# Expert rows gathered and scattered over 128 partitions instead of 96, with the slots permuted

## The chip, the cores and the metric

The kernel runs on one core of a Trainium2 chip. The metric is the device time of one execution in microseconds (us). Engines are named as in the profile: PE (TensorE), DVE (VectorE), ACT (ScalarE), POOL (GpSimd) and SP (SyncE, which here only issues DMAs). A core has 16 DMA engines; DMAs that SP issues go over one queue (q1, hardware), those of GpSimd over another (q0, software).

## What is computed

One step of a decoder layer: sparse attention and pooling over 528 prompt rows and 8 sample rows, then a mixture of experts. The change touches only the experts. 520 rows (tokens) of 1024 float32 values go to 4 of 32 experts each, so an expert gets 65 rows on average:

```python
logits = (x @ w_router).astype(jnp.float32) + b_router.astype(jnp.float32)
top_v, top_e = lax.top_k(logits, TOP_EXPERTS)          # 4 of 32
gates = jax.nn.softmax(top_v, axis=-1)
...
gu = xe @ w_gu[e] + b_gu[e]                            # 1024 -> 2048
gate = jnp.minimum(gu[:, :D_EXPERT], SWIGLU_LIMIT)
up = jnp.clip(gu[:, D_EXPERT:], -SWIGLU_LIMIT, SWIGLU_LIMIT)
act = (up + 1.0) * gate * jax.nn.sigmoid(SWIGLU_ALPHA * gate)
return act @ w_down[e] + b_down[e]
...
y = jnp.zeros((N + 1, D_MODEL), jnp.float32).at[slot_tok].add(yb.astype(jnp.float32) * slot_gate[:, None])[:N]
```

Everything is float32. The weights of one expert are 12 MB (six ring loads of 2048 KB).

## The kernel before, in words

The instructions of each engine are written out by hand, one function per engine, and tied by semaphores (`S[...]`). After attention and the output projection, the normalised rows lie in memory as `h_rows`, and the residual rows, to which the experts' results are added, as `y_acc`. Then the 32 experts follow one another; two sets of buffers (`u` = 0, 1) alternate.

**Slots.** An expert has room for 96 rows (`CAP`) in 128 slots (`SLOTS`): `iota_b` holds, for each column, which place in the expert's list that column stands for; columns 96 to 127 repeat places 64 to 95. `compare` (VectorE) sets `iota_b` against the place of each token in the expert's list, and `pick` (PE, L1250) multiplies the result with token numbers and gates, so that each partition gets the token number and the gate of its slot. `slot_rows` makes the row index out of it (`idx_i`, partitions 0 to 95); an unused slot gets an index above 519. Places are handed out from 0 up, so an expert with 65 tokens fills slots 0 to 64.

**Rows.** `gather` (POOL, L640) fetches the rows of `h_rows` for the next expert, `xg[u][0:96]`, skipping indices above 519. `turn_rows` (VectorE, L1672) turns them to `hTe`, the stationary operand. The result, `ysc[u][0:96]`, is added to `y_acc` by an indirect DMA with addition (POOL, L657), with the indices that `keep` has saved as `idx_y`. The last expert is not scattered but added by a matmul with `back` (`last_rows`, from `idx_f`). The first gather stands alone ahead of the first expert, and PE turns its rows (`turn_rows_first`, L1280).

**One expert on PE** (`pair`): `gu_round` three times (gate and up columns, L1294), with `pick` for the next expert behind the first round; two transposes (L1327, L1338); `down_wide` and `down_rest` (L1301, L1307). The groups of slots in a round are 32 wide: group 0 is partitions 0 to 31, group 1 32 to 63, group 2 64 to 95; the fourth quarter of a bank computes other columns for group 2, and so needs the gates of group 2 on partitions 96 to 127 as well.

**SP's queue** (`load`) issues, in the order in which PE sets the ring slots free: ring slots 0 and 1 (or `ring_more`), 2, 3, then the bias rows of the next expert, then slots 4 and 5. The bias rows go to four partitions, 6 KB each, L444:

```python
sp.dma_start(b_rows[0:P:GRP, :], b_gu[bass.ds(e, 1)].rearrange("a j x -> (a j) x")).then_inc(S["b_rows_in"], 16)
```

On VectorE, `pair` begins with the wait for these bias rows, and the comparison for the next expert stands behind it:

```python
dve.wait_ge(S["b_rows_in"], (ne + 1) * 16)
compare(e + 1, 1 - u)
```

and on PE `pick` waits for `cmp_ready` of that comparison before the second round can start.

Of the kernel before, what the change touches and what calls it, by code (L numbers as in the profile page):

```python
# [21 lines left out]
ALU = mybir.AluOpType  # L22
# [5 lines left out]
P = 128  # L28
# [6 lines left out]
NQ = NT - META  # L35
# [14 lines left out]
CAP = 96  # L50
SLOTS = 128
GRP = 32
# [23 lines left out]
def build_step(nc, xT, xnat, consts, g_mix, w_mt, w_v, w_mix, pool_scale, w_bra, w_brp, w_out,  # L76
# [4 lines left out]
    with ctx:  # L81
        def sb(name, shape, dt=F32):
            return ctx.enter_context(nc.sbuf_tensor(name, shape, dt))

        def sem(name):
            return ctx.enter_context(nc.semaphore(name))

        def dram(name, shape, dt=F32):
            return nc.dram_tensor(name, shape, dt).ap()

        y_acc = dram("y_acc", (NQ + CAP, D))
        h_rows = dram("h_rows", (NQ + CAP, D))
# [21 lines left out]
        idx_i = [sb(f"idx_i{n}", [P, 1], I32) for n in range(2)]  # L114
        idx_y = [sb(f"idx_y{n}", [P, 1], I32) for n in range(2)]
# [18 lines left out]
        def part(region, at, *shape):  # L134
            n = int(np.prod(shape))
            v = region[:, at:at + n]
            names = "abcd"[:len(shape)]
            if len(shape) == 1:
                return v
            return v.rearrange(f"p ({' '.join(names)}) -> p {' '.join(names)}", **dict(zip(names[1:], shape[1:])))  # L140
# [6 lines left out]
        iota96 = cst[:, C_IOTA:C_IOTA + CAP]  # L147
# [67 lines left out]
        def xn(t):  # L215
            return part(QK, D * t, D) if t < 4 else part(VN, 0, D)
# [22 lines left out]
        xg = [part(X1, D * n, D) for n in range(2)]  # L239
        ysc = [part(X1, D * (2 + n), D) for n in range(2)]  # L240
# [4 lines left out]
        iota_b = part(XR, 2048, SLOTS)  # L245
# [32 lines left out]
        def bank(n, w=512, at=0):  # L278
            return PSF[:, 512 * n + at:512 * n + at + w]
# [33 lines left out]
        scat = [sem(f"scattered{n}") for n in range(2)]  # L313
# [24 lines left out]
        def link(eng, ins, name, count):  # L338

            count[0] += 1  # L340
            ins.then_inc(S[name], 1)
            eng.wait_ge(S[name], count[0])
# [173 lines left out]
        def _(po):  # L516
# [120 lines left out]
            def gather(b, e, u):  # L637
                po.wait_ge(S["idx_ready"], b * SELS + e + 1)
                po.sem_inc(S["may"], 1)
                po.indirect_dma_start(xg[u][0:CAP], None, h_rows, bass.IndirectOffsetOnAxis(ap=idx_i[u][0:CAP, :], axis=0),  # L640
                                      bounds_check=NQ - 1, oob_is_err=False)\
                    .then_inc(gath[u], 16)

            def pair(b, i, first=False, last=False):
                for u in range(2):
                    e = i * 2 + u
                    gather(b, e + 1, 1 - u)
                    if u == 0:
                        po.wait_ge(scat[1], (b * (NE // 2) + i + (1 if first else 0)) * 16)
                    else:  # L650
                        po.wait_ge(scat[0], (b * (NE // 2) + i + 2) * 16)
                    if last and u == 1:
                        continue
                    po.wait_ge(S["idx_kept"], b * SELS + e + 1)
                    po.wait_ge(S["y_ready"], b * NE + e + 2)
                    po.sem_inc(S["may"], 1)
                    po.indirect_dma_start(y_acc, bass.IndirectOffsetOnAxis(ap=idx_y[u][0:CAP, :], axis=0),  # L657
                                          ysc[u][0:CAP], None, bounds_check=NQ - 1, oob_is_err=False, compute_op=ALU.add).then_inc(scat[u], 16)

            def experts(b, first=False):  # L660
                gather(b, 0, 0)
# [5 lines left out]
            def last_pair():  # L667
                pair(0, NE // 2 - 1, True, True)
# [718 lines left out]
        def _(dve):  # L1387
            n = [0]
            L = lambda ins: link(dve, ins, "dve_step", n)
# [149 lines left out]
            def norm_rows(n):  # L1539
                t = WO_ORDER[n]  # L1540
                r = TROWS[t]
                dve.wait_ge(S["row_ms"], 2 * n + 2)
                L(dve.reciprocal(rms[0:r, t:t + 1], rms[0:r, t:t + 1]))
                dve.scalar_tensor_tensor(out=hf(t)[0:r], in0=xn(t)[0:r], scalar=rms[0:r, t:t + 1], in1=gffn[0:r],
                                         op0=ALU.mult, op1=ALU.mult).then_inc(S["hf_done"], 1)
# [29 lines left out]
            for o, t in enumerate(WO_ORDER):  # L1575
                j, r = J_WO + o, TROWS[t]
                dve.wait_ge(S["proj_done"], j + 1)
                if t < 4:
                    x1 = xn(t).rearrange("p (a b) -> p a b", a=2)
                    dve.tensor_tensor(x1, PB[j % 2], x1, ALU.add).then_inc(S["dve_taken"], 1)  # L1580
                else:
                    for q in range(3):
                        x1 = xn(t)[0:r, 256 * q:256 * q + 256]
                        dve.tensor_tensor(x1, PB[j % 2][32 * q:32 * q + r, 0, 0:256], x1, ALU.add)
                    x1 = xn(t)[0:r, 768:D]
                    dve.tensor_tensor(x1, PB[j % 2][96:96 + r, 0, 0:256], x1, ALU.add).then_inc(S["dve_taken"], 1)
                if o == 0:
                    dve.wait_ge(S["late_in"], 48)
                    L(dve.memset(rt_log, 0.0))
                    L(dve.memset(posv, -1.0))  # L1590
                    L(dve.memset(gx, 0.0))
                    L(dve.tensor_copy(gx[:, :, 0:NE, 0], tokid[:, 0:1].unsqueeze(2).broadcast_to([P, NTILE, NE])))
                    for t_ in range(1, NTILE):
                        L(dve.memset(gx[:, t_, 0:NE, 1], float(t_)))
                    L(dve.memset(gx[:, :, 0:NE, 2], 1.0))
                if o == NTILE - 1:
                    L(dve.tensor_copy(iota_b[:, 0:CAP], iota96))
                    L(dve.tensor_copy(iota_b[:, CAP:SLOTS], iota96[:, 64:CAP]))
                norm_rows(o)
                for m in ((), (), (0,), (1,), (2, 3))[o]:  # L1600
                    find(m)
                    add_before(m)
# [6 lines left out]
            def gates():  # L1609
                dve.tensor_tensor(rt_w, top_v[:, :, 0:TOPE], top_v[:, :, 0:1].broadcast_to([P, NTILE, TOPE]), ALU.subtract).then_inc(S["sel_ready"], 1)  # L1610
                slot_rows(1, 0)
                add_before(NTILE - 1)
                dve.wait_ge(S["sel_ready"], 2)
                L(dve.tensor_reduce(sum4, rt_w, AX.X, ALU.add))
                L(dve.reciprocal(sum4, sum4))
                L(dve.tensor_tensor(rt_w, rt_w, sum4.unsqueeze(2).broadcast_to([P, NTILE, TOPE]), ALU.mult))
                L(dve.tensor_tensor(rt_eg, rt_eq, rt_w.unsqueeze(3).broadcast_to([P, NTILE, TOPE, NE]), ALU.mult))
                dve.tensor_reduce(rt_g, rt_eg.rearrange("p t k e -> p t e k"), AX.X, ALU.add).then_inc(S["g_ready"], 1)
                dve.wait_ge(S["g_ready"], 1)
                L(dve.tensor_copy(gx[:, :, 0:NE, 3], rt_g))  # L1620
                L(dve.tensor_tensor(rt_eg[:, :, 1, :], rt_g, gx[:, :, 0:NE, 3], ALU.subtract))
                L(dve.tensor_copy(gx[:, :, 0:NE, 4], rt_eg[:, :, 1, :]))
                dve.tensor_tensor(gx[:, :, 0:NE, 5], rt_eg[:, :, 1, :], gx[:, :, 0:NE, 4], ALU.subtract).then_inc(S["gx_ready"], 1)
                dve.wait_ge(S["acc_init"], 16 * 2 * NTILE)
                dve.memset(b_rows, 0.0).then_inc(S["zero_late"], 1)
                dve.memset(act_t[1][64:P], 0.0).then_inc(S["zero_late"], 1)
                dve.wait_ge(S["gate_picked"], 1)
                dve.tensor_reduce(gcol[0], bank(RANK, 3, 200), AX.X, ALU.add).then_inc(S["gcol_set"], 1)
                L(dve.tensor_reduce(rt_cnt[0:1, 0:1], bank(RANK, NE, NE * NTILE)[0:1], AX.X, ALU.max))
                dve.tensor_copy(cnt_i[0:1, 0:1], rt_cnt[0:1, 0:1]).then_inc(S["cnt_ready"], 1)  # L1630
                dve.wait_ge(S["gT_turned"], 1)
                dve.tensor_copy(back[CAP:P, 0:4, :], bank(2)[CAP:P].rearrange("p (t x) -> p t x", t=4))
                dve.tensor_copy(back[CAP:P, 4, :], bank(7, P)[CAP:P]).then_inc(S["gT_done"], 1)
                dve.tensor_copy(iota_row[:, 0:CAP], iota96)
                L(dve.tensor_scalar(iota_row[:, CAP:P], iota96[:, 0:P - CAP], float(CAP), None, ALU.add))
# [246 lines left out]
```

## Time and profile before

| what | value |
|---|---|
| median of 3 runs | 1640.55 us (1640.05 to 1643.41) |
| the profiled execution | 1642.56 us, span 1640.8 us |
| PE busy | 1596.3 us, 97% |
| DVE, ACT, POOL busy | 775.4, 273.2, 203.4 us |
| DMA | 505.80 MB, mean 308 GB/s; 378 to 399 GB/s in slices 15 to 38 |
| granted TensorE clock | 0.989 on average |
| L1294, PE, 6144 matmuls | 908.6 us |

The page gives for each engine its busy time; 40 slices of the span; the queues; the chain that ended last, followed back from the last instruction; and the costliest groups of instructions with the idle time before them. The experts run from about 540 to 1617 us. In the traces' DMA answers a queue's line reads: packets, MB, and the time of its packets as a share of 16 engines' time in the window.

### The profile page before, as it was taken

How to read it: one execution, taken by the hardware profiler on the slowest of the kernel's cores; microseconds unless marked ns; L12 is line 12 of the kernel's file. 1: busy time of each engine (PE TensorE's matmuls, PEld its weight loads, DVE VectorE, ACT ScalarE, POOL GpSimd, SP SyncE). 2: the span in 40 equal slices, each digit the busy share in tenths (PEclk: the TensorE clock that was granted, in tenths of full speed). 3: DMA queues.
4: the chain of work that ended last, by engine and by line, in shares of the span. 5: the costliest groups of instructions: out<-in, count | busy, mean ns of one | idle time of the engine just before them, and what ended most of it. 6: DMA issues, size and time to landing. Idle time of an engine off the chain costs nothing.

```text
span 1640.8 us, 33032 instructions
## 1 busy us (share of the span) xinstructions
PE 1596.3 (97%) x13471; PEld 757.4 (46%) x13471; DVE 775.4 (47%) x1615; ACT 273.2 (17%) x558; POOL 203.4 (12%) x269
## 2 busy tenths in 40 slices
PE   9999999999998999999999999999999999999997
PEld 7677487786745333333333333333333333333332
DVE  4359549403315544454445444453444535444455
ACT  2310120016112111111111111111111111111113
POOL 3624300015000000000000000000000000000000
PEclk9999999999998899999999999999999999999998
DMA  7456746622454799999999999999999999999982
GB/s 247 140 173 216 235 148 219 207 72 88 173 206 159 254 387 390 396 391 399 386 383 398 391 384 393 382 395 387 378 392 386 387 393 387 388 398 394 385 339 106
DMA packets 70669, 505.80 MB, mean 308 GB/s; under 512 B 12530, under 2 KB 12978, under 8 KB 45387
## 3 DMA queue, kind: packets, MB, share of 16 engines
q1 hardware_dynamic: 60338, 485.32, 76.2%
q0 software_dynamic: 10272, 19.72, 4.8%
q8 instruction: 35, 0.57, 0.1%
q14 instruction: 24, 0.19, 0.0%
HBM read 491.61 MB, written 21.98 MB: 313 GB/s over the span
## 4 chain that ended last, share of the span: by engine, by line
PE 68%; DMA 26%; DVE 2%; issue 1%; SPq 1%; ACT 1%; DVEq 0%; POOLq 0%; ACTq 0%
PE PS L1294 30%; DMA region_experts<-b_gu 26%; PE PS L903 16%; PE PS L1217 3%; PE PS L1301 3%; PE PS L954 2%; PE PS L1019 2%; PE PS L1307 2%; DVE region_experts L1645 1%; PE PS L1327 1%; PE PS L1250 1%; PE PS L1005 1%; PE PS L1069 1%; PE PS L1129 1%; PE PS L1114 1%
## 5 line engine op out<-in xcount | busy, mean ns | idle before, releaser
L1294 PE MATMUL PS<-weight_ring,region_experts 128*32 128x512 f32 x5376 | 680.2, 595 | 0.6 <-ACT region_experts L825 0.6
L1294 PEld LDWEIGHTS PS<-weight_ring,region_experts 128*32 128x32 f32 x5376 | 200.9, 110 | 334.3 <-issue 328.6
L1301 PE MATMUL PS<-weight_ring,act_turned 128*32 128x512 f32 x2048 | 231.4, 592 | 0.0
L1294 PE MATMUL PS<-ring_more,region_experts 128*32 128x512 f32 x768 | 228.4, 593 | 0.0
L903 PE MATMUL PS<-region_x,region_w 128*128 128x260 f32 (+1 forms) x928 | 209.4, 385 | 1.0 <-DVE region_x L1512 1.0
L903 PEld LDWEIGHTS PS<-region_x,region_w 128*128 128x128 f32 x928 | 175.6, 190 | 32.7 <-issue 4.6
L1672 DVE STREAM_TRANSPOSE region_experts<-region_x 32x256 f32<-32x256 f32 x384 | 166.8, 434 | 4.9
L1645 DVE TENSOR_TENSOR region_experts<-region_experts,region_x 128x640 bf16<-128x640 f32 x33 | 27.2, 826 | 238.8 <-DMA region_experts<-b_gu 238.5
L657 POOL DMA_INDIRECT y_acc<-region_x,idx_y x31 | 45.2, 1457 | 751.3 <-ACT region_x L856 726.0
L1301 PEld LDWEIGHTS PS<-weight_ring,act_turned 128*32 128x32 f32 x2048 | 66.7, 110 | 139.3 <-issue 133.9
L1307 PE MATMUL PS<-weight_ring,act_turned 128*32 128x256 f32 x2048 | 128.9, 381 | 0.0
L1706 DVE TENSOR_TENSOR region_experts<-PS,region_w 64x512 f32<-64x512 f32 x32 | 21.8, 682 | 180.6 <-PE PS L1294 180.6
L1307 PEld LDWEIGHTS PS<-weight_ring,act_turned 128*32 128x32 f32 x2048 | 63.6, 110 | 70.9 <-issue 43.6
L1294 PEld LDWEIGHTS PS<-ring_more,region_experts 128*32 128x32 f32 x768 | 60.1, 110 | 66.3 <-issue 66.3
L1697 DVE TENSOR_TENSOR region_x<-PS,region_w 128x512 f32<-128x512 f32 x32 | 22.1, 692 | 114.0 <-PE PS L1294 114.0
L1440 DVE MAX8 smalls<-weight_ring 8x8 f32<-8x1025 f32 (+4 forms) x96 | 71.6, 746 | 3.2
L640 POOL DMA_INDIRECT region_x<-h_rows,idx_i x33 | 32.8, 993 | 300.6 <-DVE idx_i L1662 225.8
L1441 DVE MATCH_REPLACE8 weight_ring<-smalls,weight_ring 8x1025 f32<-8x1025 f32 (+4 forms) x96 | 69.9, 728 | 0.0
L837 ACT ACTIVATE act_turned<-PS 128x384 f32<-128x384 f32 x32 | 15.7, 490 | 322.1 <-PE PS L1327 322.1
L1685 DVE STREAM_SHUFFLE region_w<-region_experts 128x1536 f32<-128x1536 f32 x32 | 60.5, 1890 | 0.0
L834 ACT ACTIVATE region_w<-region_experts 128x512 f32<-128x512 f32 x32 | 20.2, 630 | 239.1 <-DVE region_experts L1690 239.1
L1217 PE MATMUL PS<-weight_ring,region_h 128*128 128x512 f32 x128 | 55.6, 594 | 1.5 <-DVE region_h L1537 1.5
(289 smaller groups left out, 1328.5 us busy)
## 6 DMA issues: line engine op xcount, KB each, us to landing
weight_ring<-w_gu SPq DMA_DIRECT2D x112, 2048.0 KB, 18.7
weight_ring<-w_down SPq DMA_DIRECT2D x64, 2048.0 KB, 18.5
ring_more<-w_gu SPq DMA_DIRECT2D x16, 2048.0 KB, 22.0
region_w<-w_mt SPq DMA_DIRECT2D x33, 512.0 KB, 4.2
weight_ring<-cache_kT SPq DMA_DIRECT2D x64, 256.0 KB, 4.0
weight_ring<-cache_v SPq DMA_DIRECT2D x64, 256.0 KB, 4.1
weight_ring<-w_out SPq DMA_DIRECT2D x2, 2048.0 KB, 10.1
weight_ring<-bias_strip SPq DMA_DIRECT2D x1, 2560.0 KB, 13.0
```

Of the source, the lines that this page charges most:

```text
L657: po.indirect_dma_start(y_acc, bass.IndirectOffsetOnAxis(ap=idx_y[u][0:CAP, :], axis=0), ysc[u][0:CAP], None, bounds_check=NQ - 1, oob_is_ ...
L903: mm = pe.matmul(PB[j % 2][:, a, 0:width], lhs(k), rhs(k)[:, width * a:width * a + width], start=(k == 0), stop=(k == nk - 1))
L954: mm = pe.matmul(PB[j % 2][:, a, 0:HALF], wring[:, n % 4, P * k:P * k + P], hk(k)[:, HALF * a:HALF * a + HALF], start=(k == 0), stop=(k == ...
L1217: mm = pe.matmul(PB[(J_WO + n) % 2][:, a, :], sga[:, k, rows_of(t)], wo[a][:, k, :], start=(k == 0), stop=(k == KD - 1))
L1294: mm = pe.matmul(out[GRP * j:GRP * j + GRP], hTe[u][:, k, GRP * g:GRP * g + GRP], weights(c, u)[:, k, :], start=(k == 0), stop=(k == KD - 1))
L1301: pe.matmul(bank(3)[GRP * j:GRP * j + GRP], actT[:, k, GRP * g:GRP * g + GRP], w_dn[:, k, 512 * q:512 * q + 512], start=(k == 0), stop=(k ...
L1307: mm = pe.matmul(bank(4, 256)[GRP * j:GRP * j + GRP], actT[:, k, GRP * g:GRP * g + GRP], w_dn[:, k, 256 * q:256 * q + 256], start=(k == 0) ...
L1440: L(dve.max(out=max8[0:rows], in_=sc))
L1441: L(dve.match_replace(out=sc, in_to_replace=max8[0:rows], in_values=sc, imm_value=TAKEN))
L1645: dve.tensor_tensor(cmpm[u], iota_b.unsqueeze(1).broadcast_to([P, NTILE, SLOTS]), posv[:, :, bass.ds(e, 1)].broadcast_to([P, NTILE, SLOTS] ...
L1672: ins = dve.transpose(hTe[u][32 * q:32 * q + 32, :, GRP * g:GRP * g + GRP], rows[GRP * g:GRP * g + GRP, :, 32 * q:32 * q + 32])
L1685: dve.stream_shuffle(b_wide.rearrange("p r x -> p (r x)"), b_rows, [0] * GRP).then_inc(S["b_wide_done"], 1)
```

## The change

Gather and scatter name all 128 partitions of `xg`, `ysc` and the index tiles. The index of partitions 96 to 127 is set once to 648 (`NQ + P`), which is out of bounds, so these rows are skipped; the same partitions of `ysc` are set to zero once. The columns of `iota_b` are permuted: partitions 0 to 31 hold the odd places below 64, partitions 64 to 95 the even ones, partitions 32 to 63 the places from 64 on, and 96 to 127 repeat the group on 64 to 95. Within a group of 32, partition 4a + b holds the place number 8b + a of that group, so that neighbouring places lie four partitions apart.

```diff
@@ gather @@
-                po.indirect_dma_start(xg[u][0:CAP], None, h_rows, bass.IndirectOffsetOnAxis(ap=idx_i[u][0:CAP, :], axis=0),
+                po.indirect_dma_start(xg[u][:, :], None, h_rows, bass.IndirectOffsetOnAxis(ap=idx_i[u][:, :], axis=0),
                                       bounds_check=NQ - 1, oob_is_err=False)\
@@ scatter @@
-                    po.indirect_dma_start(y_acc, bass.IndirectOffsetOnAxis(ap=idx_y[u][0:CAP, :], axis=0),
-                                          ysc[u][0:CAP], None, bounds_check=NQ - 1, oob_is_err=False, compute_op=ALU.add).then_inc(scat[u], 16)
+                    po.indirect_dma_start(y_acc, bass.IndirectOffsetOnAxis(ap=idx_y[u][:, :], axis=0),
+                                          ysc[u], None, bounds_check=NQ - 1, oob_is_err=False, compute_op=ALU.add).then_inc(scat[u], 16)
@@ VectorE, last of the five row tiles @@
-                    L(dve.tensor_copy(iota_b[:, 0:CAP], iota96))
-                    L(dve.tensor_copy(iota_b[:, CAP:SLOTS], iota96[:, 64:CAP]))
+                    for q, of in enumerate((iota96[:, 1:64:2], iota96[:, 64:CAP], iota96[:, 0:64:2], iota96[:, 0:64:2])):
+                        L(dve.tensor_copy(iota_b[:, GRP * q:GRP * q + GRP].rearrange("p (a b) -> p a b", a=8),
+                                          of.rearrange("p (b a) -> p a b", a=8)))
+                    for u in range(2):
+                        L(dve.memset(idx_i[u][CAP:P, :], NQ + P))
+                        L(dve.memset(idx_y[u][CAP:P, :], NQ + P))
@@ VectorE, gates() @@
                 dve.wait_ge(S["gate_picked"], 1)
+                dve.memset(ysc[0][CAP:P], 0.0)
+                dve.memset(ysc[1][CAP:P], 0.0)
```

PE's instructions and their order are the same. On POOL the order is the same, and the gathers are wider. POOL's queue from the first gather into the loop (`region_x<-h_rows` is a gather, `y_acc<-region_x` a scatter), before:

```order
L640 DMA region_x<-h_rows,idx_i 96x1024
L649 ISA
L654 REGISTER_ALU
L657 DMA y_acc<-region_x,idx_y 616x1024
L638 REGISTER_ALU
L640 DMA region_x<-h_rows,idx_i 96x1024
```

and changed:

```order
L640 DMA region_x<-h_rows,idx_i 128x1024
L649 ISA
L654 REGISTER_ALU
L657 DMA y_acc<-region_x,idx_y 616x1024
L638 REGISTER_ALU
L640 DMA region_x<-h_rows,idx_i 128x1024
```

The gather names 128 rows instead of 96; the scatter's row shows its target only, `y_acc`, and reads the same.

On DVE, ahead of the last row tile's normalisation (`region_experts<-cst` is `iota_b`), the difference is this piece:

```order
 L1580 TENSOR_TENSOR region_qk<-PS,region_qk 128x1024
-L1597 COPY region_experts<-cst 128x96
-L1598 COPY region_experts<-cst 128x32
+L1598 COPY region_experts<-cst 128x32 x4
+L1601 MEMSET idx_i 32x1
+L1602 MEMSET idx_y 32x1
+L1601 MEMSET idx_i 32x1
+L1602 MEMSET idx_y 32x1
 L1543 RECIPROCAL smalls<-smalls 128x1
```

Six more instructions stand ahead of the reciprocal that the normalised rows, and with them the first expert, depend on.

## Rows read from the trace of the kernel before

**Rows 1.** The page: busy time of PE and others; the chain by line

```profile
PE 1596.3 (97%) x13471; PEld 757.4 (46%) x13471; DVE 775.4 (47%) x1615; ACT 273.2 (17%) x558; POOL 203.4 (12%) x269
...
PE PS L1294 30%; DMA region_experts<-b_gu 26%; PE PS L903 16%; PE PS L1217 3%; PE PS L1301 3%; PE PS L954 2%; PE PS L1019 2%; PE PS L1307 2%; DVE region_experts L1645 1%; PE PS L1327 1%; PE PS L1250 1%; PE PS L1005 1%; PE PS L1069 1%; PE PS L1129 1%; PE PS L1114 1%
```

**Rows 2.** List of waits: who waited for whom, us in total, times, longest

```profile
DVE region_experts L1645 <- DMA region_experts<-b_gu: 238.5, 30, 9.1
...
PE PS L1250 <- DVE region_experts L1645: 16.1, 25, 1.2
```

**Rows 3.** Chain that ended last, 1015 to 1050 us: start, us, what

```profile
1014.87 0.84 DVE region_experts L1645
...
1031.86 16.41 DMA region_experts<-b_gu
...
1048.41 0.84 DVE region_experts L1645
```

**Rows 4.** Timeline of PE, four selections: start, us, instruction, idle before

```profile
548.83 0.28 PE L1250 MATMUL PS<-choices,region_experts 128*128 x5
...
581.55 0.28 PE L1250 MATMUL PS<-choices,region_experts 128*128 x5
...
745.27 0.69 PE L1250 MATMUL PS<-choices,region_experts 128*128 x5
...
1591.23 0.28 PE L1250 MATMUL PS<-choices,region_experts 128*128 128x6 bf16 x5 [1.01 <-DVE region_experts L1645]
```

**Rows 5.** DMA queues, 745.27 to 1591.23 us: packets, MB, share of 16 engines

```profile
DMA packets 27493, 329.22 MB, mean 389 GB/s; under 512 B 4948, under 2 KB 4948, under 8 KB 8234
...
q1 hardware_dynamic: 21865, 316.10, 94.0%
q0 software_dynamic: 5624, 13.06, 6.2%
```

**Rows 6.** Hardware queue, 661 to 668 us, then 655 to 660 us

```profile
q1 hardware_dynamic: 201, 3.00, 100.6%
...
q1 hardware_dynamic: 93, 1.39, 84.8%
```

**Rows 7.** One scatter: slices of 1 us from 647.6, 651.6 and 652.6

```profile
DMA packets 58, 0.35 MB, mean 352 GB/s; under 512 B 29, under 2 KB 29, under 8 KB 39
...
q0 software_dynamic: 12, 0.05, 24.5%
...
q0 software_dynamic: 12, 0.01, 4.8%
```

**Rows 8.** L640 (gather) and L657 (scatter): ns min/median/max; landing; the first gather's chain

```profile
L640 POOL DMA_INDIRECT region_x<-h_rows,idx_i x33: 972/977/1443, 532.6 to 1595.6; - x33
...
DMA to landing us min/median/max: 4.5/10.8/12.2
...
L657 POOL DMA_INDIRECT y_acc<-region_x,idx_y x31: 1437/1448/1719, 577.8 to 1586.4; - x31
...
532.58 4.54 DMA region_x<-h_rows,idx_i
```

**Rows 9.** Timeline: a gather on POOL, and DVE turning its rows

```profile
1020.17 0.98 POOL L640 DMA_INDIRECT region_x<-h_rows,idx_i  x1 [7.13 <-DVE idx_i L1662]
...
1034.90 1.32 DVE L1672 STREAM_TRANSPOSE region_experts<-region_x 32x256 f32<-32x256 f32 x3
```

**Rows 10.** Timeline of DVE ahead of the first expert and in its first round

```profile
516.65 0.18 DVE L1598 COPY region_experts<-cst 128x32 f32<-128x32 f32 x1
518.12 0.16 DVE L1543 RECIPROCAL smalls<-smalls 128x1 f32<-128x1 f32 x1 [1.28 <-ACT smalls L814]
...
538.51 0.48 DVE L1626 MEMSET region_experts<- 64x512 f32 x1 [0.16 <-issue]
...
542.00 1.87 DVE L1685 STREAM_SHUFFLE region_w<-region_experts 128x1536 f32<-128x1536 f32 x1
548.96 0.69 DVE L1688 TENSOR_TENSOR region_experts<-PS,region_w 128x512 f32<-128x512 f32 x1 [5.09 <-PE PS L1294]
```

## The prediction

> **What bounds the kernel now.** I read the page first. TensorE is busy for 97% of the span, yet 26% of the chain that ended last is one small DMA, the load of an expert's bias rows (`region_experts<-b_gu`) [rows 1]. So there are two bounds close together. The list of waits says where they meet: in the expert phase TensorE waits at one place only, the slot selection at L1250, for VectorE's comparison at L1645, and VectorE waits there for that bias load [rows 2]. The chain of one expert closes as a loop: comparison, selection, TensorE's rounds, SyncE's issue, 16.4 us until the bias rows land, comparison [rows 3]. The bias load moves 24 KB; what it waits for is its place behind the weights in the DMA rings.
>
> The starts of the selections give the two speeds. In the first experts one follows the other after 32.72 us with TensorE never idle; that is TensorE's own time for an expert. From 745.27 to 1591.23, 25 experts, it is 33.84 us each. From 581.55 to 1591.23 there are 30 periods, 1009.7 us, against 30 x 32.72 = 981.6: **28.1 us are lost to the DMA** [rows 4]. It is more than the 16.1 us of waiting in rows 2, because after a wait the selection and the refilling of TensorE's pipeline take longer too. 30 x (33.84 - 32.72) would be 33.6; the missing 5.5 us are a lead that the transfers start with and use up first.
>
> **What a DMA engine does in 33.84 us.** Hardware queue: 316.10 MB in 25 experts, 12.64 MB each [rows 5]. In a stretch without row traffic it moves 3.00 MB in 7 us [rows 6], so this takes 29.5 us. Rows: 6.2% of 16 engines over 845.96 us is 839 engine-us, 33.6 per expert; 13.06 MB are 127.5 rows of 4 KB per expert, some 64 gathered and 64 scattered [rows 5]. One row costs 0.263 engine-us, a filled slot (gathered once, scattered once) 0.53. The third part is that weights run slower beside a gather: from 655 to 660 us the hardware queue holds 84.8% of the engines' time and moves only 1.39 MB, where the quiet stretch would have needed 3.26 of those 4.24 us [rows 6]. That is 1.0 us per expert on each engine. Bias rows: 6 KB on each of four engines, if each row goes to one, 0.2 us.
>
> How are the rows dealt to the engines? An expert has 225 packets on GpSimd's queue (5624 / 25) [rows 5], which is 2 x (96 + 16), so unused slots make packets too, of a few bytes. The filled slots are the lowest numbers. In the slices of one scatter 29 tiny packets come in the first us, and rows go on for five us, until the share of GpSimd's queue falls from 24.5% to 4.8% [rows 7]. All its slices hold about 0.26 MB, some 63 rows. Four rows on each of 16 engines would have ended earlier, after four turns of some 0.94 us (a row and a weight packet); five to six turns is what **six consecutive slots per engine** gives (96 / 16), with eleven engines full and five empty. Then a full engine needs 29.5 + 6 x 0.53 + 1.0 + 0.2 = 33.9 us, against 33.84 measured. The sum closes, and it says that the fullest engines bound the phase.
>
> **The change, part by part.**
> 1. Slots are permuted: odd slots of the first 64 on partitions 0 to 31, even ones on 64 to 95, slots 64 and up spread over 32 to 63 one group of four at a time, none on 96 to 127. What this brings depends on how 128 partitions are dealt, and no row shows it: this program issues no 128-row transfer from GpSimd. Bounds: dealt by fours out of each block of 32 (or one by one), an engine has 4 rows up to 64 tokens, 5 at 72, 6 at 80; I take 4.75 as the average of the fullest engine, an estimate from the mean of 64. That saves 1.25 x 0.53 = 0.66 us: 33.2 us. If each engine then also stays on its own share of the partitions and the slowdown beside the gather goes, 1.0 more: 32.2 us. Dealt by eights in a row, the engines of both full blocks have 8 rows: 33.84 + 2 x 0.53 = 34.9 us. I take the first kind. The rows that lean this way: a scatter, which only reads SBUF, and the wide loads alone run at full rate, and only the gather, which writes rows dealt by sixes, slows the loads; so loads of all 128 partitions seem to keep out of each other's way, and 128 rows may be dealt like them. It is an inference, hence its chance below.
>  The Trainium skill, DMA: Bandwidth & Descriptors, section The descriptor swizzle, says that a transfer to 128 partitions from GpSimd gives each engine four partitions of one block of 32 and four of the next; by it the sum is the one with 4 to 5 rows. Nothing in this trace shows it.
> 2. With D the engines' time for an expert, the loss is 30 x (D - 32.72) less the 5.5 us of lead, not under zero. D = 33.2: 8.9 us, a gain of 19. D up to 32.9: no loss, a gain of 28.1. Between the ends I take D near 32.9 and leave 2 us for experts with more than 72 tokens: **26 us gained**. More is not to be had: then TensorE's 32.72 us is the bound.
> 3. 32 more packets per DMA (288 per expert instead of 224), each of a few bytes like the others: 64 tiny packets over 16 engines, under 0.1 us per expert.
> 4. GpSimd names 128 rows: 977 and 1448 ns now [rows 8]; from nothing up to a third more, 0.3 and 0.5 us. It is hidden: a gather issued at 1020.17 lands 10.8 us later, and VectorE turns its rows from 1034.90 on [rows 8, 9], 4 us of cover; a scatter has most of two experts. Only the first gather is on the chain, for 4.54 us [rows 8]: 0 to +0.4 us, minus a little for fewer rows in a queue. I take +0.2.
> 5. VectorE before the first expert: four copies and four small memsets for two copies, which end at 516.83 now, with 1.28 us of idling for ScalarE's square root behind them [rows 10]. The copy of 32 columns takes 0.18 us; six more such instructions at 0.2 us with their links end at 518.0, where 518.12 is due: 0 to +0.3 us if the reordered reads are slower. I take +0.1.
> 6. Two memsets of 32x1024 after the gates: 64x512 takes 0.48 us, so 1.9 us in all. VectorE is done at 543.9 with its work before the first bank and idles 5.09 us until 548.96 [rows 10]. Free; without that cover it would cost 1.9 us once.
>
> Sum: -28.1 + 2 + 0.3, about **-26 us**. The profiled execution (1642.56, its span 1640.8) would become 1616.6, the median of the runs shown, 2.0 us below it, 1614.5.
>
> **Rivals.**
> - **Dealt by eights: slower.** The rule "96 / 16 = six in a row" that the trace shows carries on as 128 / 16 = eight in a row. Then D is 34.9, the loss 30 x 2.18 - 5.5 = 59.9 instead of 28.1, and the time is 1672. It decides as soon as the fullest engine has more than six rows. For it: the sixes just read from the slices. Against: the wide loads' full rate. Chance 0.18.
> - **Only the count of rows helps.** The slowdown beside the gather stays and the experts above 72 tokens put five and six rows back on the four engines that carry the bias rows: D 33.2 to 33.4, gain 13 to 19, 1622 to 1628. Chance 0.17.
> - **The memory is the bound, not an engine.** Then the same bytes take the same time wherever they go: 1641, with the 0.3 us of the start. For it: weights slow down on all engines beside a gather. Against: 428 GB/s in the quiet stretch (3.00 MB in 7 us) beside 389 on average [rows 5, 6]. Chance 0.07. The Trainium skill, same page, section Where 436 GB/s comes from, puts the memory's limit at some 358 GB/s per core and says it binds; by that rule nothing would be gained. The trace, at 428, is above it.
> - **The change doesn't do what it says** (packets stay 224, or the unused rows make full ones): 32 full rows more per DMA would add two per engine, as bad as the first rival. The tiny packets in the first slice [rows 7] speak against; within its 0.18.
>
> **How the numbers follow.** Gain near 26: 0.58; gain 13 to 19: 0.17; nothing: 0.07; slower: 0.18. A measurement of this kernel tells 0.2%, 3.3 us, from no change. Faster 0.75, same 0.07, slower 0.18. The range starts at the full 28.1 us with a little of the noise, 1611, and runs through the partial case to no change, 1641; the slower rival is what it leaves out. The likeliest case alone: 1611 to 1622.
>
> **What the profile would show.** Selections 32.7 to 32.9 us apart through all experts and no wait of TensorE at the selection, or its sum under 5 us; the bias load landing in under 16.5 us; 288 packets per expert; in a scatter's slices the rows gone after about four turns, not six; and, if the second half of the saving is real, hardware traffic beside a gather above 1.39 MB in 5 us. Periods near 35 us with a bias load of 18 us would mean eights. I am wrong in size if the periods stay at 33.2 or more, wrong in kind if the row count per engine falls and the period does not.

## The result, and the profile after

The changed kernel takes **1612.47 us** (median of 4 runs, 1612.01 to 1613.02) against 1640.3 us of the kernel before (median of 4 runs, 1638.31 to 1643.41). The ratio is 0.9829, 95% interval 0.9812 to 0.9846: 27.8 us less. The profiled execution took 1612.91 us, with a span of 1611.2.

Where did the time go? The chain that ended last, on the page of the changed kernel, by engine and by line:

```profile
PE 96%; DVE 1%; ACT 1%; DMA 1%; issue 1%; SPq 0%; POOLq 0%; DVEq 0%; ACTq 0%
PE PS L1294 42%; PE PS L903 16%; PE PS L1301 14%; PE PS L1307 7%; PE PS L1217 3%; PE PS L954 2%; PE PS L1019 2%; PE PS L1338 1%; PE PS L1327 1%; PE PS L1129 1%; PE PS L1005 1%; PE PS L1069 1%; PE PS L1114 1%; PE PS L968 1%; PE PS L1141 1%
```

The bias load, 26% of the chain before [rows 1], is gone from it. The stretch that answers to [rows 3] is TensorE alone; the chain of the changed kernel over one expert (start, us, what):

```profile
1005.95 0.21 PE PS L1250 x5
1006.16 12.15 PE PS L1294 x112
...
1031.81 6.87 PE PS L1294 x64
1038.67 0.21 PE PS L1250 x5
```

From selection to selection 32.72 us. The same holds for all 30 periods: the timeline of PE in the changed kernel, second and last selection, the rows that answer to [rows 4]:

```profile
580.53 0.28 PE L1250 MATMUL PS<-choices,region_experts 128*128 x5
...
1562.12 0.28 PE L1250 MATMUL PS<-choices,region_experts 128*128 128x6 bf16 x5
```

981.6 us for 30 periods, which is 30 x 32.72 to the tenth; nothing is lost to the DMA. TensorE waits for no comparison any more, and the entry of [rows 2] for VectorE has shrunk from 238.5 us. What ended the idle time ahead of the comparison (L1651 now) in the changed kernel:

```profile
  DMA region_experts<-b_gu: 27.0, 30
```

The DMA side, two stretches of the changed kernel that answer to [rows 6]: the hardware queue from 660 to 667 us, without row traffic, then both queues from 654 to 659 us, beside a gather (packets, MB, share of 16 engines):

```profile
q1 hardware_dynamic: 202, 2.97, 98.9%
...
q1 hardware_dynamic: 130, 1.93, 90.3%
q0 software_dynamic: 119, 0.21, 11.1%
```

A useful number is MB per microsecond of queue time, that is MB / (us x share). Quiet: 2.97 / (7 x 0.989) = 0.429. Beside the gather: 1.93 / (5 x 0.903) = 0.427, the same. Before it was 0.426 quiet and 1.39 / (5 x 0.848) = 0.328 beside the gather [rows 6]. So the second half of the change's saving, which the prediction only held possible, is there: **the weights are no longer slowed beside a gather**. These are single windows; the count over all gathers of a trace stands under "Gather and scatter apart".

The rows of a scatter in the changed kernel, slices of 1 us from 646.6, 647.6, 648.6 and 649.6 us (compare [rows 7]):

```profile
q0 software_dynamic: 16, 0.07, 32.9%
...
q0 software_dynamic: 49, 0.12, 61.3%
...
q0 software_dynamic: 62, 0.07, 36.9%
...
q0 software_dynamic: 8, 0.01, 4.7%
```

Some 0.27 MB (0.26 before) are nearly all through after three slices, where [rows 7] show rows up to the fifth. An expert has 288 packets on this queue, as 2 x (128 + 16) asks (window 645.97 to 678.69 us):

```profile
q0 software_dynamic: 288, 0.57, 6.6%
```

### The profile page after: what moved, and what is told of

Read it like the earlier page. It is cut to its first block, busy times and chain, and to the rows that moved or that the text cites. A ratio compares the mean times of both kernels' runs of the same rounds, so it can differ in the third digit from the quotient of the medians.

```text
span 1611.2 us, 33040 instructions
## 1 busy us (share of the span) xinstructions
PE 1582.0 (98%) x13471; PEld 732.4 (45%) x13471; DVE 778.8 (48%) x1623; ACT 273.3 (17%) x558; POOL 209.8 (13%) x269
## 3 DMA queue, kind: packets, MB, share of 16 engines
q0 software_dynamic: 12320, 19.73, 4.8%
HBM read 495.93 MB, written 26.04 MB: 324 GB/s over the span
## 4 chain that ended last, share of the span: by engine, by line
PE 96%; DVE 1%; ACT 1%; DMA 1%; issue 1%; SPq 0%; POOLq 0%; DVEq 0%; ACTq 0%
PE PS L1294 42%; PE PS L903 16%; PE PS L1301 14%; PE PS L1307 7%; PE PS L1217 3%; PE PS L954 2%; PE PS L1019 2%; PE PS L1338 1%; PE PS L1327 1%; PE PS L1129 1%; PE PS L1005 1%; PE PS L1069 1%; PE PS L1114 1%; PE PS L968 1%; PE PS L1141 1%
## 5 line engine op out<-in xcount | busy, mean ns | idle before, releaser
L1294 PEld LDWEIGHTS PS<-weight_ring,region_experts 128*32 128x32 f32 x5376 | 188.5, 110 | 345.7 <-issue 339.8
L903 PEld LDWEIGHTS PS<-region_x,region_w 128*128 128x128 f32 x928 | 175.2, 190 | 33.1 <-issue 4.6
L657 POOL DMA_INDIRECT y_acc<-region_x,idx_y x31 | 49.2, 1587 | 783.0 <-ACT region_x L856 706.1
L1694 DVE TENSOR_TENSOR region_experts<-PS,region_w 128x512 f32<-128x512 f32 x32 | 22.1, 692 | 166.7 <-PE PS L1294 166.7
L1294 PEld LDWEIGHTS PS<-ring_more,region_experts 128*32 128x32 f32 x768 | 56.6, 110 | 69.7 <-issue 69.7
L640 POOL DMA_INDIRECT region_x<-h_rows,idx_i x33 | 34.9, 1058 | 231.5 <-DVE idx_i L1668 161.5
L903 PE MATMUL PS<-weight_ring,region_w 128*128 128x260 f32 x224 | 51.1, 385 | 0.0
```

Of the source, the lines that this page charges most:

```text
L640: po.indirect_dma_start(xg[u][:, :], None, h_rows, bass.IndirectOffsetOnAxis(ap=idx_i[u][:, :], axis=0), bounds_check=NQ - 1, oob_is_err=F ...
L903: mm = pe.matmul(PB[j % 2][:, a, 0:width], lhs(k), rhs(k)[:, width * a:width * a + width], start=(k == 0), stop=(k == nk - 1))
L1294: mm = pe.matmul(out[GRP * j:GRP * j + GRP], hTe[u][:, k, GRP * g:GRP * g + GRP], weights(c, u)[:, k, :], start=(k == 0), stop=(k == KD - 1))
```

## The experiments

TensorE hides the DMA in the changed kernel, so its period says only that the DMA needs no more than about 32.9 us. To see the DMA's own time, six kernels of this study leave out blocks k = 6 and 7 of 8 of the down projection (the weights are still loaded, so the DMA traffic is whole, but the result lacks a quarter of the down projection and is wrong). They are called light here:

```diff
-                                  start=(k == 0), stop=(k == KD - 1))
+                                  start=(k == 0), stop=(k == KD - 3))
...
-                    down_wide(range(4, KD))
-                    down_rest(range(4, KD)).then_inc(S["down_done"], 1)
+                    down_wide(range(4, KD - 2))
+                    down_rest(range(4, KD - 2)).then_inc(S["down_done"], 1)
```

Their first periods, with the lead still there, are 31.14 us: TensorE's pace, more than the 30.2 expected mostly because it now waits 0.8 us per expert for VectorE to turn the rows. The light kernels ran once each. Any period above is the DMA's. I give the mean of the last 21 periods, from selections that the timeline shows.

### before_light, the yardstick

> The kernel before with blocks 6 and 7 of 8 of the down projection left out, so that TensorE needs about 30.2 us per expert (32.72 less a quarter of the 10.3 us of L1301 and L1307) and only the DMA can set the period. Balance theory (the fullest engine: 29.5 us of weights + 6 filled slots x 0.53 + 1.0 beside the gather + 0.2) and the rival (the memory's rate sets it) both expect 33.8 us between selections, as in the kernel before: this run is the yardstick for the next.

Timeline of PE in before_light, eleventh and last selection:

```profile
879.43 0.55 PE L1250 MATMUL PS<-choices,region_experts 128*128 x4 [0.57 <-DVE region_experts L1645]
...
1591.39 0.29 PE L1250 MATMUL PS<-choices,region_experts 128*128 128x6 bf16 x5 [3.73 <-DVE region_experts L1645]
```

(1591.39 - 879.43) / 21 = **33.90 us**. Less work on TensorE bought nothing (1641.2 us in one run): once its lead was used up, the kernel before was bound by its DMA through all experts. This is the sum of the prediction, 33.9.

### after_light, the DMA time that the change leaves

> The changed kernel with the same blocks left out: it shows the DMA's own time for an expert, which TensorE hides in the changed kernel. Balance alone: 33.2 us between selections. Balance and own partitions (each engine's rows lie on partitions that its weight packets write, so the weights are no longer slowed beside a gather): 32.2 us. Rival, the memory's rate: 33.8 us, which the 32.72 us of the changed kernel already contradict. Rows dealt by eights: 34.9 us.

```profile
859.83 0.58 PE L1250 MATMUL PS<-choices,region_experts 128*128 x4 [0.29 <-DVE region_experts L1651]
...
1532.02 0.28 PE L1250 MATMUL PS<-choices,region_experts 128*128 128x6 bf16 x5 [0.99 <-DVE region_experts L1651]
```

672.19 / 21 = **32.01 us** (one run, 1580.2 us). Balance alone (33.2) is too little; balance and own partitions (32.2) is right within 0.2 us. The memory's rate is out, and so are eights: with them 8 rows would lie on the fullest engines, and even without the slowdown that is 29.5 + 8 x 0.53 + 0.2 = 33.9 us. The change takes 1.9 us of DMA time from every expert, of which the full kernel can use 1.1 before TensorE bounds it.

### names_only: 128 partitions without the permutation

```diff
-                    for q, of in enumerate((iota96[:, 1:64:2], iota96[:, 64:CAP], iota96[:, 0:64:2], iota96[:, 0:64:2])):
-                        L(dve.tensor_copy(iota_b[:, GRP * q:GRP * q + GRP].rearrange("p (a b) -> p a b", a=8),
-                                          of.rearrange("p (b a) -> p a b", a=8)))
+                    L(dve.tensor_copy(iota_b[:, 0:CAP], iota96))
+                    L(dve.tensor_copy(iota_b[:, CAP:SLOTS], iota96[:, 64:CAP]))
```

> The change without the permutation: 128 partitions named, slots 0 to 95 on partitions 0 to 95 in order. Whether dealt by fours or by eights, the first 64 partitions put 8 rows on each of eight engines. Balance alone: 33.84 + 2 x 0.53 = 34.9 us per expert, 1672 us. Balance and own partitions, with fours: the 1.0 us beside the gather goes, 33.9 us per expert, 1641 us, no change against before. With eights the slowdown would stay: 34.9 us and 1672 us.

1639.45 us (median of 10 runs), ratio to the kernel before 0.9989, 95% interval 0.9973 to 1.0005: no change. Timeline of PE, eleventh and last selection:

```profile
879.29 0.55 PE L1250 MATMUL PS<-choices,region_experts 128*128 x4 [0.67 <-DVE region_experts L1650]
...
1590.33 0.28 PE L1250 MATMUL PS<-choices,region_experts 128*128 128x6 bf16 x5 [0.68 <-DVE region_experts L1650]
```

711.04 / 21 = 33.86 us, where 33.9 was expected of two effects that cancel: eight rows instead of six on the fullest engines, and no slowdown beside the gather. The second can be read directly, 1056.5 to 1061.5 us:

```profile
q1 hardware_dynamic: 132, 1.92, 89.5%
```

1.92 / (5 x 0.895) = 0.429, the quiet rate, although all rows lie on the first 80 partitions at most. So it is not the spreading of the rows that frees the weights, it is that 128 partitions are named.

This run also speaks on the deal. Dealt one by one (partition modulo 16), or in fours that go once through 64 partitions, 64 rows would be 4 on every engine, and the kernel would have been as fast as the change. It was not: the first 64 partitions share eight engines.

### order_only: the permutation with 96 partitions

The reverse of names_only: the three lines of the permutation put into the kernel before.

> The change's permutation alone, gather and scatter still on 96 partitions. Six consecutive partitions per engine then put 6 rows on the engines of partitions 0 to 29 and 66 to 95, and the weights stay slowed beside the gather: 33.8 us per expert as before, 1640 us. If the order of the slots were what helps, it would come near 1612 us.

1635.54 us (median of 10 runs), ratio 0.9971, interval 0.9958 to 0.9983: small, but clear of no change. Its selections at 878.63 and 1586.06 us give 33.69 us per expert, and 23.3 us of 28.1 are still lost. The expectation of no change was off by some 4 us, and I have not separated why. Beside its gather (1054.9 to 1059.9 us) the weights are slowed, 1.59 / (5 x 0.891) = 0.357:

```profile
q1 hardware_dynamic: 109, 1.59, 89.1%
```

The window of [rows 6] gave 0.328, but that difference is one of windows: over all gathers the two kernels are alike (table below). Neither half of the change is worth more than 5 us alone. Together they are worth 27.8.

### even_sixes: balance without naming 128

Gather and scatter stay on 96 partitions, six in a row per engine, and the slots are permuted so that each six holds four of the first 64:

```diff
-                    L(dve.tensor_copy(iota_b[:, 0:CAP], iota96))
-                    L(dve.tensor_copy(iota_b[:, CAP:SLOTS], iota96[:, 64:CAP]))
+                    L(dve.tensor_copy(iota_b[:, 0:CAP].rearrange("p (e r) -> p e r", r=6),
+                                      iota96.rearrange("p (r e) -> p e r", r=6)))
+                    L(dve.tensor_copy(iota_b[:, CAP:SLOTS], iota_b[:, 64:CAP]))
```

> 96 partitions as before, but the slots permuted so that each engine's six consecutive partitions hold four of the first 64 slots, and slots 64 to 79 give each engine one more: balance without own partitions. Balance alone suffices: about 4.6 slots on the fullest engine, 29.5 + 2.4 + 1.0 + 0.2 = 33.1 us per expert, 30 x 0.4 - 5.5 = 6.5 us lost of 28.1, 1619 us. If own partitions made most of the gain: 33.5 us or more, 1630 us or more. If the six-in-a-row deal is wrong: no change, 1640 us.

1611.3 us (median of 4), ratio 0.9826, interval 0.9807 to 0.9846: as fast as the change, better than the 1619 expected, and every period is 32.72 us. It bears out the six-in-a-row deal for 96 partitions: a permutation made for just that deal removes the whole loss. Why 33.1 us per expert was too much, its light version shows.

> The kernel with 96 partitions and even sixes, blocks 6 and 7 of 8 of the down projection left out: the DMA's own time for an expert. It needs at most some 32.9 us, since its full version loses nothing to the DMA. If crossing (an engine writing rows on partitions that another engine's weights go to) is what slows the weights beside a gather, the 1.0 us stays: 33.1 us between selections. If what matters is only that the rows are spread over all partitions instead of the lower half, the 1.0 us goes here too: 32.1 us.

Timeline of PE in even_sixes_light, eleventh and last selection, and its hardware queue beside a gather, 1042.5 to 1047.5 us:

```profile
870.08 0.58 PE L1250 MATMUL PS<-choices,region_experts 128*128 x4 [0.82 <-DVE region_experts L1646]
...
1558.30 0.28 PE L1250 MATMUL PS<-choices,region_experts 128*128 128x6 bf16 x5 [1.81 <-DVE region_experts L1646]
```

```profile
q1 hardware_dynamic: 103, 1.54, 85.8%
```

688.22 / 21 = **32.77 us**, between both expectations. The rate over this window is 1.54 / (5 x 0.858) = 0.359: in 4.29 us of queue time 3.62 would have done, so 0.7 us are lost instead of 1.0, and the sum 29.5 + 2.4 + 0.7 + 0.2 is 32.8. The slowdown is not milder for that. The rows of this gather fill only some 3.2 of the 5 us; where they are, from 1043 to 1046 us, the rate is 0.80 / (3 x 0.795) = 0.335:

```profile
q1 hardware_dynamic: 54, 0.80, 79.5%
```

Evenly dealt rows are through sooner, and so the weights are slowed for a shorter time. Balance alone is worth 1.1 us per expert (33.90 - 32.77): some 0.7 for fewer rows on the fullest engine and 0.3 for the shorter gather. That is what the full kernel can use (33.84 - 32.72). The other 0.8 us of the change's 1.9 are a reserve behind TensorE.

### Gather and scatter apart

```diff
-                po.indirect_dma_start(xg[u][:, :], None, h_rows, bass.IndirectOffsetOnAxis(ap=idx_i[u][:, :], axis=0),
+                po.indirect_dma_start(xg[u][0:CAP], None, h_rows, bass.IndirectOffsetOnAxis(ap=idx_i[u][0:CAP, :], axis=0),
```

> The changed kernel with the gather back on 96 partitions (slots permuted as in the change, so six consecutive partitions per engine; the scatter stays on 128), same blocks of the down projection left out. The changed kernel took 31.9 us per expert in this state. Gather rows cost some 0.2 us each: 1.25 more on the fullest engine is 0.25 us. Balance alone expects 32.1 us. If the gather's place matters, up to 1.0 us more: 33.1 us.

> The changed kernel with the scatter back on 96 partitions (six consecutive per engine, gather on 128), same blocks left out. Scattered rows cost some 0.33 us each, 1.25 more on the fullest engine is 0.4 us: 32.3 us. Nothing else is expected, as the weights were not slowed beside a scatter. If balance is not what matters: 31.9 us.

(scatter96_light does the same to the scatter.) Last selections of gather96_light, then of scatter96_light; the eleventh ones are at 871.10 and 862.30 us:

```profile
1569.38 0.29 PE L1250 MATMUL PS<-choices,region_experts 128*128 128x6 bf16 x5 [2.97 <-DVE region_experts L1651]
...
1544.96 0.28 PE L1250 MATMUL PS<-choices,region_experts 128*128 128x6 bf16 x5 [1.20 <-DVE region_experts L1651]
```

With the gather on 96 partitions it is 698.28 / 21 = 33.25 us, 1.24 more than after_light (32.01; the 31.9 in the expectation was 0.1 too low): the 33.1 of the theory in which its place matters, not the 32.1 of balance alone. Beside that gather (1044.9 to 1049.9 us) the rate is down again:

```profile
q1 hardware_dynamic: 109, 1.65, 91.7%
```

1.65 / (5 x 0.917) = 0.360. With the scatter on 96 it is 682.66 / 21 = 32.51 us, 0.5 more where 0.4 was expected of balance. The slowdown belongs to the gather.

Single windows of 5 us depend on how much of them a gather fills. The packed traces hold every packet, so the reading can be made for all gathers issued from 740 to 1520 us (23 or 24 in each kernel). The weights travel in packets of 16 KB; at the quiet rate one takes 611 ns. The table has those that start between the first and the last row of a gather. Lost is their time above 611 ns, per gather and engine.

| kernel | gather names | its rows take, us (median) | 16 KB packet, ns (median) | lost, us |
|---|---|---|---|---|
| before | 96 | 5.3 | 782 | 0.97 |
| before_light | 96 | 5.4 | 782 | 0.99 |
| order_only | 96 | 5.2 | 777 | 0.92 |
| gather96_light | 96 | 5.2 | 761 | 0.90 |
| even_sixes | 96 | 3.8 | 814 | 0.76 |
| even_sixes_light | 96 | 3.8 | 799 | 0.72 |
| names_only | 128 | 5.5 | 611 | 0.00 |
| scatter96_light | 128 | 3.3 | 611 | 0.00 |
| after | 128 | 3.1 | 611 | 0.01 |
| after_light | 128 | 3.4 | 611 | 0.00 |
| flat_light | 128 | 3.3 | 611 | 0.01 |

The kernels fall into two classes by the number of partitions that the gather names, and by nothing else in the table: not by the order of the slots, not by how long the rows take, not by the scatter. The prediction's 1.0 us, taken from one window, is also the mean over all gathers (0.97).

### flat_light: how 128 partitions are dealt

The change without the spreading inside a group of 32: neighbouring slots on neighbouring partitions.

```diff
-                        L(dve.tensor_copy(iota_b[:, GRP * q:GRP * q + GRP].rearrange("p (a b) -> p a b", a=8),
-                                          of.rearrange("p (b a) -> p a b", a=8)))
+                        L(dve.tensor_copy(iota_b[:, GRP * q:GRP * q + GRP], of))
```

> The changed kernel without the spreading inside the groups of 32 (neighbouring slots on neighbouring partitions), same blocks left out. Dealt by fours, slots 64 to 67 all fall on the first engine, which also carries bias rows: 8 rows there for every expert with 68 or more tokens (29.5 + 8 x 0.53 + 0.2 = 33.9 us), 4 for one with up to 64 (31.8 us), on average some 32.7 us and uneven from expert to expert. Dealt one by one (partition modulo 16): 5 rows at most, 32.1 us and even.

The mean is (1545.76 - 861.96) / 21 = 32.56 us, and the periods differ. Timeline of PE in flat_light:

```profile
1059.84 0.28 PE L1250 MATMUL PS<-choices,region_experts 128*128 x5
...
1090.99 0.68 PE L1250 MATMUL PS<-choices,region_experts 128*128 x5
...
1122.60 0.58 PE L1250 MATMUL PS<-choices,region_experts 128*128 x4
...
1156.11 0.58 PE L1250 MATMUL PS<-choices,region_experts 128*128 x4 [1.85 <-DVE region_experts L1650]
```

31.15 us (TensorE's pace, no wait), then 33.51 us two experts on. The mean is that of **fours** (32.7 expected; one by one 32.1). The unevenness alone would be weak ground, since the last 21 periods of after_light also go from 31.14 to 33.28 us; but one by one is excluded by names_only too.

The scatters' lengths count the rows on the fullest engine a third way. From the first row to the last but two, a scatter takes (median of 22 to 24) 6.3 us in names_only, where the deal puts 8 rows there; 4.8 to 4.9 us in before_light and scatter96_light, with 6; and 3.3 us in after_light and even_sixes_light, with 4 to 5.

Four partitions of one block of 32 and four of the next is also what the Trainium skill, DMA: Bandwidth & Descriptors, section The descriptor swizzle, says of a transfer to 128 partitions; these runs agree with it for an indirect one. No record names the engine of a packet, so the deal is inferred from periods and lengths, not seen.

### Again side by side, and one small thing

> The 96-partition version with even sixes again, beside the changed kernel on the same chip. Its DMA time of 32.8 us per expert is just above TensorE's 32.72, which the lead covers, and it has none of the change's memsets (0.3 us at the start) and a shorter first gather (0.4 us): 0.5 to 1.2 us below the changed kernel, 1611.5 us.

> The changed kernel again, for comparison on the same chip: 1612.5 us.

even_sixes took 1612.73 us (5 runs, ratio 0.9835, interval 0.9816 to 0.9854), the change 1612.21 us (5 runs, 0.983, 0.9812 to 0.9849). They cannot be told apart. The 0.5 to 1.2 us expected do not show; intervals of 3 us to either side cannot exclude them.

```diff
@@ first row tile @@
+                    for u in range(2):
+                        L(dve.memset(idx_i[u][CAP:P, :], NQ + P))
+                        L(dve.memset(idx_y[u][CAP:P, :], NQ + P))
@@ last row tile @@
-                    for u in range(2):
-                        L(dve.memset(idx_i[u][CAP:P, :], NQ + P))
-                        L(dve.memset(idx_y[u][CAP:P, :], NQ + P))
```

> The changed kernel with the four index memsets moved to the first row tile, where VectorE waits for TensorE anyway: the 0.3 us at the start come back and nothing else changes: 1612.2 us. If anything else than these instructions delays the start: 1612.5 us.

1613.04 us (5 runs, ratio 0.9837, interval 0.9818 to 0.9856): no gain shows. The timeline of VectorE in the changed kernel says why, beside [rows 10]:

```profile
516.75 0.85 DVE L1598 COPY region_experts<-cst 128x32 f32<-128x32 f32 x4
517.65 0.06 DVE L1601 MEMSET idx_i<- 32x1 int32 x1
...
518.01 0.06 DVE L1602 MEMSET idx_y<- 32x1 int32 x1
518.44 0.16 DVE L1543 RECIPROCAL smalls<-smalls 128x1 f32<-128x1 f32 x1 [0.37 <-ACT smalls L814]
```

Each memset takes 0.06 us, and 0.37 us of idling for ScalarE are left. There was nothing to win back.

## Why the prediction was right, point by point

- **The number.** The range of 1611 to 1641 us ran from the full gain to no change, so that 1612.5 lies in it says little. The narrower claim, 1611 to 1622 with 26 us gained, is the one that was tested, and it held: 27.8.
- **The bound.** Right: two bounds close together, and the fullest DMA engines' time as the one that decided. before_light confirms the sum of 33.9 us with 33.90, and the values worked out the same way for names_only, after_light, scatter96_light, gather96_light and flat_light are met within some 0.2 us.
- **What the sum leaves open.** It charges every weight packet at the quiet rate, 611 ns. Even where no row packet starts within 0.8 us, the 16 KB packets of the kernel before take 636 ns in the mean (median 613), 0.7 us more per expert and engine, and the sum has no term for that. The same excess is 0.5 us in after_light, where the rows are evenly dealt, and 1.6 us in names_only, where they are dealt worst. That would fit long packets on engines that have time to spare, but no packet's record names its engine, so it stays open.
- **Loads at full rate beside a scatter.** Nearly: 625 ns in the median instead of 611, in before_light (scatter of 96) and after_light (128) alike.
- **Six consecutive slots per engine for 96 partitions.** Right; even_sixes is a permutation made for this deal, and it takes the whole loss away.
- **How 128 partitions are dealt.** The step that rested on the weakest ground, taken at 0.75 against eights at 0.18. flat_light and names_only show fours. Eights are excluded by after_light, 32.01 us where 8 rows ask for 33.9 even without a slowdown. names_only alone would not do it: both deals put 8 rows on eight engines there, and the 1672 us held against its 1639 assumed that the slowdown would stay. The ground of the choice was thin. That wide loads and scatters are not slowed does not say how 128 rows are dealt; it was a guess in the right direction.
- **D, the engines' time after the change: the mis-sized term.** The prediction took a value near 32.9 between 33.2 and 32.2; after_light measured 32.01. The slowdown beside the gather, which I had not trusted to go, went entirely (0.427 against 0.429; 0.01 us lost per gather instead of 0.97). It cost the forecast little, since below 32.9 the time does not depend on D; but the 2 us left for experts with more than 72 tokens were not lost, and that is the difference between 1614.5 and 1612.5.
- **The ceiling.** 28.1 us were said to be all there is; 27.8 came.
- **Packets.** 288 as expected, at no cost that shows.
- **Signs.** Periods of 32.72 us, no wait at the selection, 288 packets and 1.93 MB beside the gather all came as named. Rows went in fewer turns: with the DMA as the bound, the rows of a scatter take 3.3 us (after_light) instead of 4.9 (before_light).
- **GpSimd.** A gather now takes 1042 ns instead of 977, a scatter 1584 instead of 1448, well inside "up to a third more". Hidden. The first gather's piece of the chain is 4.2 to 6.4 us in six profiles with 96 partitions and 4.6 to 5.6 us in five with 128, of those that have it on the chain; +0.2 us cannot be told in that spread.
- **VectorE at the start.** Counted as +0.1 us, in truth 0: the memsets were priced at 0.2 us with links and take 0.12. The two memsets of `ysc` took 0.91 us each, as estimated, and left 2.30 us of the 5.09 us of cover.

One warning: even_sixes reaches the same time by balance alone. That the changed kernel is fast does not show that its partitions matter. The light kernels and names_only do.

## What to carry to other kernels

When a stream of loads fills the DMA engines, look at the fullest engine, not at the sum of bytes: 0.26 MB of rows per transfer, laid out by sixes on eleven of sixteen engines, cost 1.1 us per expert more than the same rows dealt evenly (before_light against even_sixes_light), beside 12.6 MB of weights. Work out how each partition count is dealt (96 here as six in a row, 128 as fours from blocks of 32) and permute the data to fit; the permutation is free where a table already sets the order, and here it was enough: two copies changed (even_sixes) gave the whole time that the change gave. And where another engine is the bound next to it, take work away from that engine for one measurement: the period then shows what the DMA needs, and how much reserve a change leaves.

## What was not expected

- A gather on 96 partitions lowers the rate of the weights beside it by a fifth to a quarter (packets of 761 to 814 ns in the median against 611), and one on 128 partitions does not slow them at all, not even with all rows on the first 80 partitions. Nine in ten of the weight packets beside a gather of 96 take over 640 ns, more than eleven of sixteen engines can account for: engines that have no rows are slowed too. The gather's own rows are slowed as well: 179 to 195 ns in the median with 96, 159 with 128. No such loss showed for a scatter on 96 (scatter96_light: 0.5 us, of which balance explains 0.4). The likely reason is that an engine then writes on partitions that belong to another engine's part of the loads; nothing here shows the write path, so this stays an inference.
- Rows of a scatter go through in bursts in the changed kernel: GpSimd's queue takes 61.3% of a slice, where [rows 7] show 24.5%. It is not the 128 partitions that do it. even_sixes, with 96, bursts too, from 647.5 to 648.5 us:

```profile
q0 software_dynamic: 31, 0.11, 57.6%
q1 hardware_dynamic: 13, 0.15, 35.8%
```

  after_light, with 128, does not (in the median scatter 40% in the fullest slice, like even_sixes_light, against 64% in the changed kernel). The kernels that burst are those in which TensorE is the bound. Perhaps their hardware queue has less waiting just then; no run tests it.
- The page's count of bytes written to memory rose from 21.98 to 26.04 MB. That is 31 scatters x 32 rows x 4 KB; the queue's own bytes did not rise (19.72 and 19.73 MB). The page's count seems to go by the rows that an instruction names, so skipped rows are in it.
